# Expert weights in units of 4 MB, with 32 KB per partition, in a ring of four units

## The reference

```python
def expert_ffn(xb, w1, b1, w2, b2):
    gu = xb @ w1 + b1
    gate, up = gu[:, :D_EXPERT], gu[:, D_EXPERT:]
    gate = jnp.minimum(gate, SWIGLU_LIMIT)
    up = jnp.clip(up, -SWIGLU_LIMIT, SWIGLU_LIMIT)
    glu = gate * jax.nn.sigmoid(gate * SWIGLU_ALPHA)
    return ((up + 1) * glu) @ w2 + b2

def layer(x, ...):
    y, vrows, conv_new = mixer(rmsnorm(x, g_mix), ...)       # w_in 1024 x 2560, w_out 1024 x 1024
    x = x + y
    x = x + cross_attn(rmsnorm(x, g_xattn), mk, mv, w_q, w_xo)
    x = x + moe(rmsnorm(x, g_moe), w_router, b_router, w1, b1, w2, b2)   # top 4 of 32 experts
    return x, vrows, conv_new
```

## Time and profile before

| | us |
|---|---|
| median of three runs | 1209.21 |
| lowest and highest | 1208.95, 1210.45 |
| the profiled execution | 1209.51 |
| its span, first to last instruction | 1207.8 |
| TensorE busy (matmuls) | 1146.7 |
| VectorE busy | 300.8 |
| ScalarE busy | 157.1 |
| SyncE's DMA queue, share of the 16 engines | 89.5% |
| moved, and mean rate | 458.25 MB, 379 GB/s |

### The profile page before, as it was taken

How to read it: one execution, slowest core, us unless ns; L and a number is a source line. 1 busy time by engine, 2 the same in 40 slices (tenths; PEclk the granted TensorE clock), 3 DMA queues, 4 the chain that set the end, 5 groups by cost and what they waited for, 6 DMA issues and landing times.

```text
span 1207.8 us, 15000 instructions
## 1 busy us (share of the span) xinstructions
PE 1146.7 (95%) x5983; PEld 618.0 (51%) x5983; DVE 300.8 (25%) x633; ACT 157.1 (13%) x243; POOL 28.1 (2%) x62
## 2 busy tenths in 40 slices
PE   8999999999999999999999999999999999999996
PEld 7888887685444444544444444344434443434444
DVE  5114532342212122222121221212121212121214
ACT  2011011031111101211010111011101110111012
POOL 0000000000000000000000000000000000000000
PEclk9999999999999999999999999999999999999999
DMA  9963344997999999999999999999999999999993
GB/s 366 393 232 139 118 156 142 427 381 284 420 428 428 429 428 428 430 427 429 429 427 429 430 427 430 428 428 429 428 429 429 428 428 429 428 428 430 428 427 123
DMA packets 38808, 458.25 MB, mean 379 GB/s; under 512 B 5856, under 2 KB 6624, under 8 KB 8064
## 3 DMA queue, kind: packets, MB, share of 16 engines
q1 hardware_dynamic: 35856, 454.11, 89.5%
q10 hardware_dynamic: 2928, 3.80, 0.9%
HBM read 454.41 MB, written 3.23 MB: 379 GB/s over the span
## 4 chain that ended last, share of the span: by engine, by line
PE 38%; DMA 31%; DVE 6%; issue 1%; DVEq 0%; ACT 0%; SPq 0%; ACTq 0%
PE ps L1186 21%; DMA ring<-in_w_gu 17%; DMA arena<-in_w_gu 14%; PE ps L1230 12%; DVE arena L880 2%; PE ps L1212 2%; PE ps L1161 2%; DVE arena L890 1%; DVE arena L893 1%; DVE arena L887 1%; PE ps L1135 0%; PE ps L1238 0%; DVE resid L908 0%; PE ps L1196 0%; DVEq L880 0%
## 5 line engine op out<-in xcount | busy, mean ns | idle before, releaser
L1186 PE MATMUL ps<-ring,arena 128*64 128x512 f32 x1536 | 341.2, 594 | 26.1 <-DMA ring<-in_w_gu 26.1
L1186 PEld LDWEIGHTS ps<-ring,arena 128*64 128x64 f32 x1536 | 109.3, 137 | 253.4 <-issue 206.1
L958 PE MATMUL ps<-arena,ring 128*128 128x264 f32 (+1 forms) x800 | 179.2, 386 | 1.4 <-issue 1.0
L1230 PE MATMUL ps<-ring,arena 128*64 128x512 f32 x768 | 170.1, 595 | 6.5 <-DVE arena L893 6.5
L859 DVE TENSOR_TENSOR resid<-resid,ps 128x264 f32<-128x264 f32 x128 | 50.1, 425 | 479.7 <-PE ps L1161 479.7
L958 PEld LDWEIGHTS ps<-arena,ring 128*128 128x128 f32 x800 | 151.6, 190 | 27.2 <-issue 1.6
L1186 PE MATMUL ps<-arena 128*64 128x512 f32 x512 | 114.0, 594 | 7.5 <-DMA arena<-in_w_gu 7.5
L1230 PEld LDWEIGHTS ps<-ring,arena 128*64 128x64 f32 x768 | 53.0, 137 | 112.4 <-issue 95.9
L1135 PE MATMUL ps<-arena 128*128 128x128 f32 x816 | 101.7, 281 | 0.0
L1135 PEld LDWEIGHTS ps<-arena 128*128 128x128 f32 x816 | 99.2, 197 | 0.0
L573 ACT ACTIVATE arena<-ps 128x1024 f32<-128x1024 f32 x32 | 32.8, 1024 | 452.8 <-PE ps L1186 452.8
(11 more groups left out here) (188 smaller groups left out, 499.6 us busy)
## 6 DMA issues: line engine op xcount, KB each, us to landing
ring<-in_w_gu SPq DMA_DIRECT2D x96, 2048.0 KB, 30.3
ring<-in_w_dn SPq DMA_DIRECT2D x48, 2048.0 KB, 35.3
arena<-in_w_gu SPq DMA_DIRECT2D x32, 2048.0 KB, 29.9
arena<-in_w_dn SPq DMA_DIRECT2D x16, 2048.0 KB, 35.3
ring<-in_w_in SPq DMA_DIRECT2D x10, 1024.0 KB, 27.8
ring<-in_kc SPq DMA_DIRECT2D x8, 1024.0 KB, 4.8
ring<-in_vc SPq DMA_DIRECT2D x8, 1024.0 KB, 5.0
ring<-in_w_v SPq DMA_DIRECT2D x4, 1024.0 KB, 23.1
```

What stands on the lines that cost most here:

```text
L958: last = mm(b[:, 0:width], w[:, k, P * (m % 2):P * (m % 2) + P], source(k), start=(k == 0), stop=(k == KT - 1))
L1186: last = mm(ps[64 * h:64 * h + 64, n, :], xg[cur][:, k, SLOTS * (i % 2):SLOTS * (i % 2) + SLOTS], w[:, at:at + 512], start=(k == 0), stop= ...
L1230: last = mm(ps[64 * h:64 * h + 64, 4, :], hid[:, k, :], w[:, at:at + 512], start=(k == 0), stop=(k == KT - 1))
```

## The change

A unit becomes 4 MB: four tiles of gate/up rows, or all eight tiles of down rows, so an expert has three units instead of six, and a partition reads 32 KB in one piece. The ring has four such units in the same 16 MB: one in `arena` (the memory of both old ones) and three in `ring`, four slots each. `chunk_slot` shifts the slots of the front chunks so that the last twelve lie in slots 0 to 11 in order. The waits before each issue follow: the first unit now waits for ("o", 7) alone, the next three each for four slots, and `next_unit` for the down unit of two experts ago, the first gate/up unit of the previous expert, or its second one. On TensorE the loops over units get longer and the waits and semaphore steps fewer (`w_used` once per expert). The strides of gather and transposes double, to 4 and 8, the bias add loses one dimension of its pattern, and the bias shuffle has 8 transfers of half the size. Where the diff leaves out hunks, only `n % RING` is replaced by `chunk_slot(n)`.

```diff
--- before.py
+++ after.py
@@ -24,10 +24,10 @@
 SLOTS = 64
 RING = 12
 SLOT = 2048
-UNITS = 6
-RING_UNITS = 8
-ROWS_GU = 2
-ROWS_DN = 4
+UNITS = 3
+RING_UNITS = 4
+ROWS_GU = 4
+ROWS_DN = 8
 EPS = 1e-5
 LIMIT = 7.0
 ALPHA = 1.702
@@ -52,6 +52,11 @@
                 + [("vc", c) for c in range(NS)] + [("w_xo", c) for c in range(4)])
 NF = len(FRONT_CHUNKS)
 CHUNK_AT = {key: n for n, key in enumerate(FRONT_CHUNKS)}
+
+
+def chunk_slot(n):
+    return (n - NF) % RING
+

@@ -179,8 +184,8 @@

         at = 20 * T
         h_tok = [view(at, D), view(at + D, D), h_last]
-        unit_at = [sq_at - 4 * SLOT, sq_at - 2 * SLOT]
-        assert at + 2 * D <= unit_at[0]
+        unit_at = sq_at - 4 * SLOT
+        assert at + 2 * D <= unit_at
         at = sq_at + 2 * T
         p_hot = view(at, TT, 2 * SLOTS)
         at += TT * 2 * SLOTS
@@ -213,7 +218,7 @@
         b_sp = par_of("b_sp").rearrange("p (m t) -> p m t", m=4)
         b_gu = par_of("b_gu").rearrange("p (e h m) -> p e h m", e=NE, h=2)
         b_tiles = par_of("b_gu").rearrange("p (j e h b) -> p j e h b", j=ROWS_DN, e=NE, h=2)
-        b_split = view(12 * T, ROWS_DN, 2 * NE, 2)
+        b_split = view(12 * T, ROWS_DN, 2 * NE, KT // ROWS_DN)
         router = par_of("router").rearrange("p (k e) -> p k e", k=KT)


@@ -313,10 +318,9 @@

         def unit_buffer(n):

-            if n < 2:
-                return arena[:, unit_at[n]:unit_at[n] + 2 * SLOT]
-            s = (NF + 2 * (n - 2)) % RING
-            return ring[:, s:s + 2, :].rearrange("p a n -> p (a n)")
+            if n == 0:
+                return arena[:, unit_at:unit_at + 4 * SLOT]
+            return ring[:, 4 * n - 4:4 * n, :].rearrange("p a n -> p (a n)")

         def columns(t, first):

...
@@ -340,40 +344,36 @@
                     continue
                 if n >= RING:
                     front_free(sp, n - RING)
-                sp.dma_start(ring[:, n % RING, :], front_dram[kind][c]).then_inc(landed[n % RING], 16)
+                sp.dma_start(ring[:, chunk_slot(n), :], front_dram[kind][c]).then_inc(landed[chunk_slot(n)], 16)

             def expert_unit(expert, number, i):
                 n = number % RING_UNITS
-                if i < 4:
-                    rows = w_gu[bass.ds(expert, 1), 2 * i:2 * i + 2].rearrange("a k p n -> (a k p) n")
+                if i < 2:
+                    rows = w_gu[bass.ds(expert, 1), 4 * i:4 * i + 4].rearrange("a k p n -> (a k p) n")
                     src = rows.rearrange("(p j) n -> p (j n)", j=ROWS_GU)
                 else:
-                    rows = w_dn[bass.ds(expert, 1), 4 * (i - 4):4 * (i - 4) + 4].rearrange("a k p n -> (a k p) n")
+                    rows = w_dn[bass.ds(expert, 1), 0:KT].rearrange("a k p n -> (a k p) n")
                     src = rows.rearrange("(p j) n -> p (j n)", j=ROWS_DN)
                 sp.dma_start(unit_buffer(n), src).then_inc(unit_landed[n], 16)

             def first_unit(n):
                 if n == 0:
-                    sp.wait_ge(grp, G["sS"] + 1)
+                    sp.wait_ge(grp, G[("o", 7)] + 1)
                     sp.wait_ge(mix_stored, 48)
-                elif n == 1:
-                    sp.wait_ge(grp, G[("o", 7)] + 1)
                     sp.wait_ge(kv_stored, 32)
                 else:
-                    front_free(sp, NF - RING + 2 * (n - 2))
-                    front_free(sp, NF - RING + 2 * (n - 2) + 1)
+                    for c in range(4 * n - 4, 4 * n):
+                        front_free(sp, NF - RING + c)
                 expert_unit(n // UNITS, n, n % UNITS)

             def next_unit(e, expert, number, i):

                 if i == 0:
-                    sp.wait_ge(w_used, e * 4 - 4)
+                    sp.wait_ge(d_done, e - 1)
                 elif i == 1:
-                    sp.wait_ge(d_done, e - 1)
-                elif i == 5:
+                    sp.wait_ge(w_used, e)
+                else:
                     sp.wait_ge(gu_done, e)
-                else:
-                    sp.wait_ge(w_used, e * 4 - 5 + i)
                 expert_unit(expert, number, i)

             for n in range(RING_UNITS):
@@ -877,9 +877,7 @@
                     gate_v, up_v = tb[:, :, 0:SLOTS], tb[:, :, SLOTS:2 * SLOTS]
                     for h in range(2):
                         bias = b_tiles[:, :, bass.ds(expert0 + i, 1), h, :].rearrange("p m a b -> p (a b) m")
-                        TTN(both[:, :, h, :].rearrange("p (b m) s -> p b m s", b=2),
-                            turned[:, :, h, :].rearrange("p (b m) s -> p b m s", b=2),
-                            bc(bias, 3, [P, 2, ROWS_DN, SLOTS]), ALU.add).then_inc(t_read, 1)
+                        TTN(both[:, :, h, :], turned[:, :, h, :], bc(bias[:, 0, :], 2, [P, KT, SLOTS]), ALU.add).then_inc(t_read, 1)
                         dve.wait_ge(t_read, e * 2 + 2 + h)
                         if h == 0:
                             TS(gate_v, gate_v, LIMIT, None, ALU.min).then_inc(g_ready, 1)
...
@@ -1128,7 +1126,7 @@
             def gather(b, n, begun=False):

                 for part in range(4):
-                    first = 512 * n + 256 * (part // ROWS_GU) + part % ROWS_GU
+                    first = 512 * n + part
                     for t in range(TT):
                         if begun:
                             pe.wait_ge(p_built if t == 2 else first_p, 1 if t == 2 else t + 1)
@@ -1175,17 +1173,17 @@
                     pe.wait_ge(gu_copied, e + 1)
                     if i % 2 == 0:
                         pe.wait_ge(side_copied, twin * 3 + 1)
-                    for u in range(4):
-                        if i == 0 and u == 2:
+                    for u in range(2):
+                        if i == 0 and u == 1:
                             pe.wait_ge(emptied, NG)
                         w = expert_unit(u)
-                        for k in (2 * u, 2 * u + 1):
+                        for k in range(4 * u, 4 * u + 4):
                             for n in range(2):
                                 for h in range(2):
-                                    at = SLOT * (k % 2) + D * h + 512 * n
+                                    at = SLOT * (k % 4) + D * h + 512 * n
                                     last = mm(ps[64 * h:64 * h + 64, n, :], xg[cur][:, k, SLOTS * (i % 2):SLOTS * (i % 2) + SLOTS],
                                               w[:, at:at + 512], start=(k == 0), stop=(k == KT - 1))
-                        last.then_inc(w_used if u < 3 else gu_done, 1)
+                        last.then_inc(w_used if u < 1 else gu_done, 1)

                     pos = twin * 3 + 2 * (i % 2)
                     if i % 2 == 0:
@@ -1222,14 +1220,13 @@
                     pe.wait_ge(hid_ready, e + 1)
                     pe.wait_ge(y_left, e + 1)
                     pe.wait_ge(y_right, e + 1)
-                    for u in range(4, UNITS):
-                        w = expert_unit(u)
-                        for k in range(4 * (u - 4), 4 * (u - 4) + 4):
-                            for h in range(2):
-                                at = D * (k % 4) + 512 * h
-                                last = mm(ps[64 * h:64 * h + 64, 4, :], hid[:, k, :], w[:, at:at + 512],
-                                          start=(k == 0), stop=(k == KT - 1))
-                        last.then_inc(w_used if u < UNITS - 1 else d_done, 1)
+                    w = expert_unit(2)
+                    for k in range(KT):
+                        for h in range(2):
+                            at = D * k + 512 * h
+                            last = mm(ps[64 * h:64 * h + 64, 4, :], hid[:, k, :], w[:, at:at + 512],
+                                      start=(k == 0), stop=(k == KT - 1))
+                    last.then_inc(d_done, 1)
             pe.wait_ge(y_left, end * 4 + 1)
             pe.wait_ge(y_right, end * 4 + 1)
             pe.wait_ge(c_added, end * 16 + 1)
```

More of the change, by code:

```diff
@@ L333, in _ @@
                 sp.dma_start(mem_raw[:, k:k_end, :], mem_t[:, k:k_end, :]).then_inc(mem_in[part], 16)
-                sp.dma_start(ring[:, 0, 256 * k:256 * k_end], w_k[0, :, 256 * k:256 * k_end]).then_inc(
-                    landed[0] if part == 2 else part_landed[part], 16)
+                sp.dma_start(ring[:, chunk_slot(0), 256 * k:256 * k_end], w_k[0, :, 256 * k:256 * k_end]).then_inc(
+                    landed[chunk_slot(0)] if part == 2 else part_landed[part], 16)
             for n, (kind, c) in enumerate(FRONT_CHUNKS):
@@ L935, in chunk @@
                 n = CHUNK_AT[key]
-                pe.wait_ge(landed[n % RING], 16 * (n // RING + 1))
-                return ring[:, n % RING, :]
+                pe.wait_ge(landed[chunk_slot(n)], 16 * (n // RING + 1))
+                return ring[:, chunk_slot(n), :]
             def sum_squares(name, n, width, token_tiles=0):
@@ L964, in _ @@
             keep_busy(ps[:, 7, :], 9)
-            first_keys = ring[:, 0, :].rearrange("p (k n) -> p k n", k=KT)
```

(3 more changed lines are left out.)

## The result

| | before | after |
|---|---|---|
| median | 1209.21 us (1208.95 to 1210.45) | 1247.53 us (1247.27 to 1247.93) |
| ratio | | 1.0318, 95% interval 1.0305 to 1.0331 |
| profiled execution, span | 1207.8 us | 1245.7 us |
| the loop's first product | 276.11 us | 281.55 us |
| an expert, once the loop runs | 27.34, then 29.37 us | 29.67 us throughout |

A forecast was written before the change was run, and what follows sets the result against it. TensorE bounds the first ten experts, then the weight stream: 1209.5 + 3.4 (restart) + 0.4 (second gap) + 3.4 (last landing) - 7.2 (rate) - 0.3 = 1209.2 us. Own range 1207.5 to 1211.5; 8-in-10 range 1207.0 to 1217.0.

The forecast's parts named there:

- small edits: Bias shuffle, bias add and the doubled strides of transposes and gathers: bounds 0 and +1 us for the strides, taken as 0.
- All three signs: Prediction wrong if loop starts after 276.5 us, a slice behind 310 us is under 420 GB/s, or rate outside 431 to 433.
- The rate: Expert weight stream: 4 MB units save 79.6 ns each over 91 units, 432.0 GB/s, -7.2 us; bounds 0 and -14.5.
- two-point line: Through the rates of 1 MB and 2 MB transfers: 2407.5 ns per MB plus 79.6 ns per transfer, assumed to hold at 32 KB.
- Rivals A: Weight stream: the rate stays at 428.5 GB/s, leaving only the costs, 1216.4 us; chance 0.30.
- B: Fixed part shrinks more than the line gives, or matmuls behind a landing are partly covered: 1202 or 1206 us; chance 0.09.
- D: Read side suffers from pieces starting 32 KB apart: by 1% of the rate, 9 us longer, 1225 us; chance 0.04.
- The restart: Loop start: first next unit issued after 32 matmuls instead of 16, at 283.16 instead of 279.73 us: +3.4 us.
- the second gap: Third next unit waits for the whole down unit; the queue runs dry, 1.3 us lost against some 0.8: +0.4 us.
- the last landing: Kernel's end: 32 matmuls instead of 16 stand behind the landing of the last gate/up unit: +3.4 us.
- The ring: Buffers in the streamed part are freed early enough, least lead 18 us against 1.65 needed: cost nothing.
- Rival C: Coarser frees leave the engines idle in each expert; one microsecond for each of 31 gives 1240 us; chance 0.03.

The follow-up runs named there:

- host_rows: The changed kernel with gate/up rows laid out on the host so that the gather reads its weight operand at stride 1: 1209.42 us, ratio 1.0003.
- pieces16: perm_turn with every 4 MB unit moved as two 2 MB transfers of 16 KB pieces, waited for together: 1217.54 us, ratio 1.0065.
- halves runs: Some units split in halves, near the restart and in late gate/up units: on perm_turn 1210.22 us, on host_rows 1206.12 us.
- before_stride4: The kernel before with only the gather's weight operand read at stride 4 in place of 2: 1249.71 us, ratio 1.0334.
- before_order: The kernel before with h_tok written by ScalarE in the gather's order, so the gather reads at stride 1 in place of 2: 1211.96 us, ratio 1.0024.
- after_order: The changed kernel with h_tok written by ScalarE in the gather's order, so the gather reads at stride 1 in place of 4: 1212.82 us, ratio 1.0029.
- perm_turn: The changed kernel with the turns of h_fm making the gather's order through a permuted identity, ScalarE's copies contiguous, gather at stride 1: 1211.90 us, ratio 1.0015.

## Why the prediction was wrong, point by point

**The step that failed** is the one I had put among the small edits: "Transposes read a stride of 8 instead of 4 and gathers of 4 instead of 2 ... Bounds 0 and +1 us; I take 0." Measured: +2.8 us for each gather, two ahead of the loop (+5.4) and one in each expert. Four faults lie in it. I read the cost of the gather's stride 4 off a transpose at stride 4 (212 ns), and a plain product at that stride loads in 329. I took the load for hidden, since an instruction of the gather came every 118 ns (24 in 2.83 us) and so faster than its own load; but with loads of 329 ns one comes every 234 ns (24 in 5.61 us), so the pace follows the load even where loads overlap. I bounded the cost for one pass, though it falls in each expert. And I wrote down TensorE's slack (27.34 against 29.13 us) without asking what uses it up: 1.8 us an expert, which a gather that takes 2.8 us longer more than fills. The expert grows by 2.33 to 29.67, less than 2.8, since TensorE had waited 0.25 to 0.32 us for the activation anyway and the transposes got shorter. So TensorE never uses up the lead of the units that were loaded ahead, and the whole loop runs at its pace. The rule of the Trainium skill that I cited beside it cut both ways, free up to 4 fp32 and dear once each access meets a new line of 16 bytes; at stride 4 only the second half came true, and I gave it no place among the rivals. All three signs that I had named came: the loop starts at 281.55, slices behind 310 us fall to 409 GB/s, and the rate from 560 to 1170 us is 425.

**The rate**: right, though the changed kernel can't show it, since TensorE holds it at 425. Whole packets there; in host_rows 431.8 GB/s against 432.0. The two-point line held at 32 KB, and pieces16 puts the loss without it at 6.6 us. Rivals A, B and D have fallen.

**The restart, the second gap, the last landing**: right in host_rows. +3.3 us (279.73 to 283.03) for 3.4; the third next unit at 303.53 for 303.84; the last wait at 1172.04 for about 1173, and 7.09 us behind it for 3.65. What I had wrong is how the two costs at the start hang together: they are one wait of the stream for TensorE, and the halves runs show that the last dry place counts, not their sum. (The 1.3 and 0.8 us of the second gap differ by 0.5, not by the 0.4 that stands in the sum.)

**The ring**: right. The 431.8 GB/s of host_rows from 600 to 1150 us leave no room for a stall in each expert. Rival C has fallen: its 1240 us came near the measured 1247.5, but by another mechanism, and before_stride4 makes the loss without coarser frees. **The first four units, b_down, the bias shuffle**: no cost seen, the loop starts at 275.97.

**The time**: 1209.2 was in effect the forecast for a kernel without this stride, and that kernel takes 1209.42. Part of so close a match is luck: the loop starts 0.14 us earlier there, the rate gives some 0.4 us less than the line, and the second gap is no term of its own.

## What to carry to other kernels

When a layout is changed to make transfers longer, list every operand whose stride changes with it, and price the stride on the same kind of instruction. For each engine write its slack under the bound, and hold every cost of unknown size against that slack and the number of times it falls. A gain of 0.8% in the stream was here worth just what the coarser units cost at its two ends; longer pieces paid here only where the ends were kept finer. When an edit leaves TensorE idle for a while, look at the granted clock behind it before putting the time down to the instructions.

## What the runs showed of the hardware

- A weight load of 128 x 128 in a plain fp32 product, at a granted clock of 1.00, takes 192 ns at stride 1, 196 at 2, 261 at 3, 329 at 4 and 334 at 8 floats. A group of 24 such instructions takes 2.68, 2.83 and 5.61 us at strides 1, 2 and 4.
- A load of 128 x 128 in a transpose: 141, 200, 212, 198 ns at 1, 2, 4, 8. In the kernels before and after, at strides 4 and 8, eight transposes take 0.97 and 0.88 us or, in every second expert, 1.24 and 1.16.
- A moving operand of 512 columns: 592, 621, 1098, 1098 ns at 1, 2, 4, 8.
- A ScalarE copy of 128 x 512 from PSUM takes 1113 ns in place of 674 when its output is written in the order of the gather, neighbours 128 floats apart.
- Behind 2.5 us of idle TensorE the granted clock fell to 0.50 for about 3 us in before_order and after_order, and a gather of stride 1 took 4.31 and 3.51 us in place of 2.68. In perm_turn it stood at 0.50 from 267 to 270 us without such an idle stretch in front.
- Pieces of 8, 16 and 32 KB per partition with 8 pieces per engine and transfer stream at 421.6, 428.5 and 431.8 GB/s; the first two give a line of 79.6 ns per transfer, which gives 432.0 for the third.
